# MLP up projections with the activations stationary, and a transposition by 32x32 blocks and DMAs

## The chip, the cores and the metric

The kernel runs on one core of one Trainium2 chip. The metric is the device time of one execution in microseconds; lower is better.

## The reference

A decoder trunk of two layers on 256 tokens of width 2048, all in float32. Layer 0 mixes with a gated linear recurrence and dilated window attention, layer 1 with differential attention. Each mixer is followed by a squared-ReLU MLP with 8192 hidden features; after each of the four sublayers comes a layer norm:

```
def squared_relu_mlp(x, w1, w2):
    h = jax.nn.relu(x @ w1)
    return (h * h) @ w2

for layer in range(DEPTH):
    ...
    x = layer_norm(ALPHA * x + mix, ln_mix_g[layer], ln_mix_b[layer])
    x = layer_norm(ALPHA * x + squared_relu_mlp(x, mlp_w1[layer], mlp_w2[layer]), ln_mlp_g[layer], ln_mlp_b[layer])
```

## The kernel before, in words

Every large product is made of three products of rounded parts. Each operand is split into a high part (the value in the matmul's float32r form) and a low part (the rest), and high x high, high x low and low x high are summed. The activations stand in SBUF with features on partitions: `xT` for the sublayer's input and `yT` for what the output products read, each with high and low parts. The first half of `yT` is `hT`, the hidden features of one block; the second half, `hT_last`, takes those of the last block.

All weights stream from HBM in blocks. A block has 8 chunks, a chunk is 256 rows by 512 columns. SyncE loads two chunks with one DMA of 1 MB into `raw`, which holds 8 chunks (`load`, line 267); the load waits until VectorE has made the low part of the chunks that lay there (`s_lo`). ScalarE makes the high part of a chunk (`split_hi`, line 364), VectorE the low part (`split_lo`, line 986), into rings of 4 chunks, `w_hi` and `w_lo`. So the high part of a chunk can be made once TensorE has finished the chunk four before it (`s_used`).

TensorE takes a chunk in one of two forms. `turned_chunk` (lines 674 and 678) holds 128x128 pieces of the weights stationary: 8 matmuls with 512 moving columns (high and low parts of the 256 tokens together) into four PSUM banks and 8 with 256 columns. Its result has features on partitions, in two halves (columns 0 to 255 and 256 to 511 of a bank) that still have to be added. `natural_chunk` (lines 700 to 702) holds 128 tokens of the activations stationary and moves 512 weight columns: 12 matmuls into two banks, one for each 128 tokens. Its result has tokens on partitions.

The MLP has 16 pairs of blocks in each layer: an up block (512 hidden features, `turned_chunk`) and a down block (`natural_chunk`, which adds the 512 features' share to all 2048 outputs). The order is up(0), then up(i+1), down(i) for i = 0 to 14, then down(15). It is written out by hand, the same for all engines: ScalarE and VectorE walk through the chunks k = 2 to 17 of up(i+1) and down(i) (`up_down`), some chunks ahead of TensorE, and other work is put at fixed k. When up(i+1) is done (k = 9), ScalarE copies the right halves from PSUM into `cross` (`copy_cross`), VectorE adds the left halves into `qs` (`add_cross`) and squares with ReLU (`squared`). At k = 4 of the next round `hidden_hi` (ScalarE, line 571) and `hidden_lo` (VectorE, line 1390) split `qs` into `hT`, before TensorE reaches the down block (chunks k = 8 to 15 of the round). After each quarter of a down block VectorE adds two banks to the residual `res` (line 1058). The first up block of a layer stands in `lead`, among the transpositions of the new `xT`. An engine executes its instructions in order, so whatever stands behind a waiting instruction waits too; this holds for SyncE's loads.

Of the kernel before, what the change touches and what calls it, by code (L numbers as in the profile page):

```python
# [70 lines left out]
GROUPS = D // CN  # L71


T_M0 = 8
T_OIN = T_M0 + FB
T_M1 = T_OIN + 2 * GROUPS


N_EOUT = 0
# [64 lines left out]
def build(nc, x, positions, ev_w_in, ev_conv_w, ev_conv_b, ev_gate_a_w, ev_gate_a_b, ev_gate_x_w,  # L144
# [11 lines left out]
    with ExitStack() as ctx:  # L156
# [3 lines left out]
        def sem(name):  # L160
# [34 lines left out]
        ln_x = ks[:].rearrange("p a s -> p (a s)").rearrange("p (b n) -> p b n", b=2)  # L195
        hT, hT_last = yT[:, 0:4], yT[:, 4:8]

        ln_par, rnn_par = rg[:, 0, 0, 0:P], rg[0:64, 0, 1, 0:P]
        pos, ang, turns = (rg[0:ROT, 1, n] for n in range(3))
        lam_vec = rg[:, 2]  # L200
# [29 lines left out]
        s_bn, s_k8, s_var, s_std, s_shift = (  # L230
            sem("block_statistics"), sem("softplus_made"), sem("variance"),
            sem("std"), sem("shift"))
        s_sq, s_hhi, s_hlo = sem("hidden_squared"), sem("hidden_hi"), sem("hidden_lo")
        s_S, s_neg, s_exp, s_P, s_T, s_pT, s_O = (sem("scores"), sem("neg_max"), sem("exps"), sem("probs"),
                                                  sem("probs_turned"), sem("probs_turned_copied"),
# [26 lines left out]
        @block.sync  # L262
        def _(sp):
            def load(blk, q, src):

                sp.wait_ge(s_lo, (blk - 1) * BLK + (2 * q + 2))
                sp.dma_start(raw[:, 2 * q:2 * q + 2].rearrange("p k t c -> p (k t) c"), src).then_inc(s_raw[q], 16)

            xv = x[0].rearrange("(t p) n -> p t n", p=P)
            sp.dma_start(cst[:, 0:P], consts[:, 0:P]).then_inc(s_id, 16)  # L270
            for k in range(BLK):
                cols = slice(k * CK * P, (k + 1) * CK * P)
                sp.dma_start(res[:, :, cols], xv[:, :, cols]).then_inc(s_x[k], 16)
                first = w_ein[k // 2, EVEN_IN_COLS[0]][:, k % 2 * CK:k % 2 * CK + CK]
                sp.dma_start(raw[:, k], first).then_inc(s_first[k], 16)
            sp.dma_start(cst[:, P:K_W], consts[:, P:K_W]).then_inc(s_cst, 16)
            for b, col in enumerate(EVEN_IN_COLS[1:], 1):
                for q in range(PAIRS):
                    load(B_EIN + b, q, w_ein[q, col])

            def load_out(order, blk, w):
                for n, (nb, kp, _, _) in enumerate(order[::2]):
                    load(blk + n // PAIRS, n % PAIRS, w[kp // 2, nb])

            def mlp(layer, b0):
                def up(blk, b):
                    for q in range(PAIRS):
                        load(blk, q, w_m1[layer][q, b])

                def down(blk, b):  # L290
                    for q in range(PAIRS):
                        load(blk, q, w_m2[layer][b, q])
                up(b0, 0)
                with sp.Fori(0, FB - 1) as i:
                    up(i * 2 + (b0 + 1), i + 1)
                    down(i * 2 + (b0 + 2), i)
                down(b0 + 2 * FB - 1, FB - 1)
# [57 lines left out]
        def _(act):  # L355
# [206 lines left out]
            layer_norm(0)  # L562


            def mlp(n, t0, b0):

                def hidden_hi(b, dst=hT):
                    act.wait_ge(s_sq, b + 1)
                    if dst is hT:
                        act.wait_ge(s_used, last_down(b))  # L570
                    nc.scalar.activation(dst[:, :, 0], qs[:], ACT.Copy).then_inc(s_hhi, 1)
# [5 lines left out]
                copy_cross(b0, t0)  # L577

                def up_down(i, last=False):

                    blk = i * 2 + (b0 + 1)
                    for k in range(2, 18):
                        split_hi(blk, k)
                        if k == 4:
                            hidden_hi(i + h0)
                        if k == 9:
                            copy_cross(blk, i + (t0 + 1))
                        if k == 12 and last:
                            hidden_hi(i + h0 + 1, hT_last)
# [12 lines left out]
            mlp(0, T_M0, B_M0)  # L602


            def odd_exps(idx):
# [54 lines left out]
                split_hi(B_OOUT, k)  # L660
                odd_events(k, 14, 12)
            layer_norm(2)
            mlp(2, T_M1, B_M1)


        @block.tensor
        def _(pe):
# [81 lines left out]
            def lead(n, blk, t):  # L749

                if n == 0:
                    ahead = 2
# [95 lines left out]
            for n, (nb, kp, first, last) in enumerate(EVEN_OUT):  # L848
# [1 line left out]
                    pe.wait_ge(s_v, 2)  # L850
                    pe.wait_ge(s_ylo, H_DIL)
                if first and nb == 1:
                    pe.wait_ge(s_turned, 2 * T_M0)
# [10 lines left out]
                even_events(B_EOUT * BLK + n)  # L864


            def mlp(n, t0, b0, n0):
                h0 = FB * (n // 2)

                def up(blk, t):  # L870
                    for k in range(BLK):
                        turned_chunk(blk, k, t)
# [13 lines left out]

                lead(n + 1, b0, t0)
                with pe.Fori(0, FB - 1) as i:
                    up(i * 2 + (b0 + 1), i + (t0 + 1))
# [3 lines left out]
            mlp(0, T_M0, B_M0, N_M0)  # L893


            def odd_scores(idx, hh, g):
# [65 lines left out]
            last_group = GROUPS - 1  # L962
            for n, (nb, kp, first, last) in enumerate(ODD_OUT):
                if n == 0:
                    pe.wait_ge(s_turned, 2 * T_M1)
# [10 lines left out]
            mlp(2, T_M1, B_M1, N_M1)  # L976


        @block.vector
        def _(dve):  # L980
# [394 lines left out]
            layer_norm(0, B_M0 * BLK)  # L1375


            def mlp(n, t0, b0, n0):
                h0 = FB * (n // 2)

                def squared(t):

                    add_cross(t, qs)
                    dve.wait_ge(s_turned, t * 2 + 2)
                    nc.vector.scalar_tensor_tensor(out=flat(qs[:]), in0=flat(qs[:]), scalar=0.0, in1=flat(qs[:]),
                                                   op0=ALU.max, op1=ALU.mult).then_inc(s_sq, 1)

                def hidden_lo(b, dst=hT):
                    dve.wait_ge(s_hhi, b + (h0 + 1))
                    nc.vector.tensor_tensor(dst[:, :, 1], qs[:], dst[:, :, 0].bitcast(F32), ALU.subtract).then_inc(s_hlo, 1)  # L1390
# [6 lines left out]
                squared(t0)  # L1397

                def up_down(i, last=False, first=False):

                    blk = i * 2 + (b0 + 1)
                    for k in range(2, 18):
                        split_lo(blk, k)
                        if k == 4:
                            hidden_lo(i)
                        if k == 9:
                            squared(i + (t0 + 1))
                        if first and k in (6, 8, 12, 14):
                            gain_residual(n, (6, 8, 12, 14).index(k))
                        if k == 12 and last:  # L1410
                            hidden_lo(i + 1, hT_last)
                        if k in (11, 13, 15, 17):
                            if first:
# [19 lines left out]
                else:  # L1433
                    last_layer_norm()

            mlp(0, T_M0, B_M0, N_M0)


            def odd_softmax(idx):
# [91 lines left out]
            mlp(2, T_M1, B_M1, N_M1)  # L1531


INPUTS = ["x", "positions", "ev_w_in", "ev_conv_w", "ev_conv_b", "ev_gate_a_w", "ev_gate_a_b", "ev_gate_x_w",
# [18 lines left out]
```

## Time and profile before

| | |
|---|---|
| median of 3 runs | 2177.41 us (2177.38 to 2177.56) |
| profiled execution, span | 2175.0 us |
| TensorE matmul busy | 2149.4 us, 99% |
| weight load busy (beside matmuls) | 1839.0 us, 85% |
| VectorE busy | 1431.8 us, 66% |
| ScalarE busy | 1021.6 us, 47% |
| DMA | 409.05 MB, mean 188 GB/s |

The span runs from the first to the last instruction of the one profiled execution; the timed runs last a little longer, since they include what lies around it. Busy shares of TensorE are of pipelined instructions, whose ends are modelled: the distance from one start to the next tells more than the duration. The page's `L` numbers are lines of the kernel.

### The profile page before, as it was taken

To read this page: it belongs to the slowest core of one execution; us is meant where nothing else is said; L and a number is where in the kernel's file an instruction comes from. 1 tells how busy PE (TensorE), PEld (TensorE's weight loads), DVE (VectorE), ACT (ScalarE), POOL (GpSimd) and SP (SyncE) were. 2 spreads that over 40 slices of the span, in tenths; PEclk is the share of its full clock that TensorE was granted. 3 is DMA by queue.
4 is the path that set the end of the run, shared out by engine and by line. 5 is a ranking of instruction groups with operands and counts; after the bars stand their busy time and mean duration, and the time that the engine had idled before them with its cause. 6 is when DMAs were issued, how large, how long until landed. Compare 5 with 4: busy or idle time off the path is not lost.

```text
span 2175.0 us, 29150 instructions
## 1 busy us (share of the span) xinstructions
PE 2149.4 (99%) x11058; PEld 1839.0 (85%) x11058; DVE 1431.8 (66%) x1480; ACT 1021.6 (47%) x1224; POOL 28.5 (1%) x38
## 2 busy tenths in 40 slices
PE   8999999999999999999999999999999999999997
PEld 7888888888888888888888888888888888888886
DVE  6776666756665666566787666567656665666667
ACT  4446656444444444444545545554444444444443
POOL 2000000000000000000000000000000000000002
PEclk9999999999999999999999999999999999999998
DMA  8555564655555555555564554555655555555552
GB/s 279 178 171 167 179 235 155 232 193 189 188 196 186 186 193 193 193 179 197 165 224 158 188 166 173 175 173 183 226 191 186 197 190 194 176 194 191 193 193 97
DMA packets 203809, 409.05 MB, mean 188 GB/s; under 512 B 6800, under 2 KB 9088, under 8 KB 202736
## 3 DMA queue, kind: packets, MB, share of 16 engines
q1 hardware_dynamic: 201920, 398.94, 54.8%
q0 software_dynamic: 1840, 9.44, 1.3%
q8 instruction: 32, 0.52, 0.1%
q14 instruction: 17, 0.14, 0.0%
HBM read 406.26 MB, written 2.10 MB: 188 GB/s over the span
## 4 chain that ended last, share of the span: by engine, by line
PE 97%; DVE 1%; DMA 1%; ACT 0%; SPq 0%; issue 0%
PE ps L674 32%; PE ps L678 17%; PE ps L701 15%; PE ps L700 15%; PE ps L702 15%; DMA raw<-in_ev_w_in 1%; PE ps L772 0%; PE ps L740 0%; PE ps L813 0%; PE ps L720 0%; PE ps L719 0%; PE ps L718 0%; PE ps L771 0%; PE ps L776 0%; DVE res L1106 0%; DVE stats L1072 0%
## 5 line engine op out<-in xcount | busy, mean ns | idle before, releaser
L364 ACT ACTIVATE w_hi<-raw 128x1024 fp32r<-128x1024 f32 x752 | 790.1, 1059 | 819.5 <-PE ps L702 479.4
L986 DVE TENSOR_TENSOR w_lo<-raw,w_hi 128x1024 fp32r<-128x1024 f32 x752 | 902.4, 1220 | 347.7 <-ACT w_hi L364 347.5
L674 PE MATMUL ps<-xT,w_hi 128*128 128x512 f32 x3072 | 769.5, 394 | 3.9 <-DVE xT L1016 3.6
L674 PEld LDWEIGHTS ps<-xT,w_hi 128*128 128x128 f32 x3072 | 557.0, 189 | 108.0 <-DVE xT L1016 4.6
L700 PE MATMUL ps<-w_hi,yT 128*128 128x512 f32 x1240 | 484.1, 390 | 0.0
L701 PE MATMUL ps<-w_lo,yT 128*128 128x512 f32 x1240 | 482.8, 389 | 0.0
L702 PE MATMUL ps<-w_hi,yT 128*128 128x512 f32 x1240 | 482.5, 389 | 0.0
L678 PEld LDWEIGHTS ps<-xT,w_lo 128*128 128x128 f32 x3072 | 408.7, 190 | 23.9
L678 PE MATMUL ps<-xT,w_lo 128*128 128x256 f32 x3072 | 420.2, 283 | 0.0
L1058 DVE TENSOR_TENSOR res<-ps,res 128x1024 f32<-128x1024 f32 x131 | 160.3, 1224 | 187.9 <-PE ps L702 187.9
L700 PEld LDWEIGHTS ps<-w_hi,yT 128*128 128x128 f32 x1240 | 232.7, 188 | 48.8
L702 PEld LDWEIGHTS ps<-w_hi,yT 128*128 128x128 f32 x1240 | 232.7, 188 | 48.6
L701 PEld LDWEIGHTS ps<-w_lo,yT 128*128 128x128 f32 x1240 | 232.8, 188 | 48.3
L993 DVE TENSOR_TENSOR qs<-ps,cross 128x512 f32<-128x512 f32 x76 | 52.6, 692 | 112.4 <-ACT cross L374 88.1
L374 ACT ACTIVATE cross<-ps 128x512 f32<-128x512 f32 x48 | 28.7, 598 | 142.1 <-PE ps L674 142.1
L700 PE MATMUL ps<-w_hi,xT 128*128 128x512 f32 x192 | 75.9, 395 | 0.0
L702 PE MATMUL ps<-w_hi,xT 128*128 128x512 f32 x192 | 74.8, 390 | 0.0
L701 PE MATMUL ps<-w_lo,xT 128*128 128x512 f32 x192 | 74.8, 390 | 0.0
L376 ACT ACTIVATE cross<-ps 128x512 f32<-128x512 f32 x48 | 28.7, 597 | 35.7 <-PE ps L674 35.7
L702 PEld LDWEIGHTS ps<-w_hi,xT 128*128 128x128 f32 x192 | 36.0, 188 | 7.7
L700 PEld LDWEIGHTS ps<-w_hi,xT 128*128 128x128 f32 x192 | 36.1, 188 | 7.5
L701 PEld LDWEIGHTS ps<-w_lo,xT 128*128 128x128 f32 x192 | 36.1, 188 | 7.4
(180 smaller groups left out, 826.2 us busy)
## 6 DMA issues: line engine op xcount, KB each, us to landing
raw<-in_mlp_w SPq DMA_DIRECT2D x256, 1024.0 KB, 5.0
raw<-in_od_w_in SPq DMA_DIRECT2D x48, 1024.0 KB, 5.1
raw<-in_ev_w_in SPq DMA_DIRECT2D x36, 1024.0 KB, 5.1
raw<-in_ev_w_out SPq DMA_DIRECT2D x16, 1024.0 KB, 5.0
raw<-in_od_w_out SPq DMA_DIRECT2D x16, 1024.0 KB, 5.0
raw<-in_ev_w_in SPq DMA_DIRECT2D x8, 512.0 KB, 11.8
res<-in_x SPq DMA_DIRECT2D x8, 256.0 KB, 9.7
rg<-in_ln_mix_g POOLq DMA_DIRECT2D x2, 1024.0 KB, 5.0
```

Source lines behind the costliest of these rows:

```text
L364: nc.scalar.activation(flat(w_hi[:, k % NSPL]), flat(raw[:, k % NRAW]), ACT.Copy).then_inc(s_hi, 1)
L374: nc.scalar.activation(cross[:, 0:2], ps[:, 0:2, S:2 * S], ACT.Copy).then_inc(s_cross, 1)
L376: nc.scalar.activation(cross[:, 2:4], ps[:, 2:4, S:2 * S], ACT.Copy).then_inc(s_cross, 1)
L674: return nc.tensor.matmul(ps[:, f], w_hi[:, k % NSPL, i, f * P:f * P + P], both, start=k == 0 and i == 0, stop=k == BLK - 1 and i == CK - 1)
L678: return nc.tensor.matmul(ps[:, f, S:2 * S], w_lo[:, k % NSPL, i, f * P:f * P + P], xT[:, CK * k + i, 0], start=False, stop=False)
L700: nc.tensor.matmul(bank, src[:, kt + i, 0, toks], hi, start=(start and i == 0), stop=False)
L701: nc.tensor.matmul(bank, src[:, kt + i, 0, toks], lo, start=False, stop=False)
L702: ins = nc.tensor.matmul(bank, src[:, kt + i, 1, toks], hi, start=False, stop=(stop and i == CK - 1))
L986: nc.vector.tensor_tensor(flat(w_lo[:, k % NSPL]), flat(raw[:, k % NRAW]), flat(w_hi[:, k % NSPL]).bitcast(F32), ALU.subtract).then_inc(s_ ...
L993: nc.vector.tensor_tensor(dst[:, 2 * h:2 * h + 2], ps[:, 2 * h:2 * h + 2, 0:S], cross[:, 2 * h:2 * h + 2], ALU.add).then_inc(s_turned, 1)
L1058: nc.vector.tensor_tensor(res[:, :, nb * CN:nb * CN + CN], ps[:, pair[0]:pair[0] + 2], res[:, :, nb * CN:nb * CN + CN], ALU.add).then_inc( ...
```

## The change

The up blocks of both MLPs use `natural_chunk` with `xT` stationary, into banks 0 and 1 (in `lead` into banks 2 and 3). The result now has tokens on partitions and hidden features along them, while the down product needs features on partitions. VectorE turns all 32x32 blocks of the two banks with one transpose instruction into `cross` (`blocks_turned`); each 32x32 block is then right in itself but stands in the wrong group of 32 partitions. SyncE exchanges the groups with 16 DMAs from SBUF to SBUF, `cross` to `ks` (`move_hidden`): each goes from one group of 32 partitions to one group, with 1 KB for each partition, written as two pieces of 512 B. Then VectorE squares `ks` into `qs`, and `hidden_hi` and `hidden_lo` split `qs` as before, reading it in pieces of 32 elements.

In the order of the work: `copy_cross` and `add_cross` go from the MLP. `blocks_turned` stands at k = 9. `move_hidden(i)` stands in SyncE's queue behind the first of the four loads of down(i). `squared(i)` moves to k = 4 of the round that has down(i), and waits there for the 16 DMAs; `hidden_hi` and `hidden_lo` move to k = 5. For the last block `squared` stands at k = 12 and the two splits at k = 13. TensorE waits before the seventh chunk of a down block until the newest block has been turned.

```
 # SyncE
+                def move_hidden(b):
+
+                    sp.wait_ge(s_block_tr, b + (layer * FB + 1))
+                    for a in range(NQ):
+                        for c in range(NQ):
+                            sp.dma_start(tiles_moved[QUAD * c:QUAD * c + QUAD, :, a],
+                                         tiles_turned[QUAD * a:QUAD * a + QUAD, c]).then_inc(s_moved, 16)
+
                 def down(blk, b):
                     for q in range(PAIRS):
                         load(blk, q, w_m2[layer][b, q])
+                        if q == 0:
+                            move_hidden(b)
 # ScalarE
                     for k in range(2, 18):
                         split_hi(blk, k)
-                        if k == 4:
+                        if k == 5:
                             hidden_hi(i + h0)
-                        if k == 9:
-                            copy_cross(blk, i + (t0 + 1))
-                        if k == 12 and last:
+                        if k == 13 and last:
                             hidden_hi(i + h0 + 1, hT_last)
 # TensorE
-                def up(blk, t):
+                def up(blk):
                     for k in range(BLK):
-                        turned_chunk(blk, k, t)
+                        natural_chunk(blk, k, (0, 1), xT, CK * k, k == 0, k == BLK - 1)
...
+                        if k == 6 and src is hT:
+                            pe.wait_ge(s_block_tr, b + (h0 + 2))
 # VectorE
-                def squared(t):
-
-                    add_cross(t, qs)
-                    dve.wait_ge(s_turned, t * 2 + 2)
-                    nc.vector.scalar_tensor_tensor(out=flat(qs[:]), in0=flat(qs[:]), scalar=0.0, in1=flat(qs[:]),
+                def blocks_turned(blk, bank):
+
+                    dve.wait_ge(s_used, blk * BLK + BLK)
+                    nc.vector.transpose(tiles_turned.rearrange("p c t f i -> p (t f) c i"),
+                                        ps[:, bank:bank + 2].rearrange("p t (f c j) -> p (t f) c j", c=NQ, j=QUAD)
+                                        ).then_inc(s_block_tr, 1)
+
+                def squared(b):
+
+                    dve.wait_ge(s_moved, (b + (h0 + 1)) * (16 * NQ * NQ))
+                    nc.vector.scalar_tensor_tensor(out=flat(qs[:]), in0=flat(ks[:]), scalar=0.0, in1=flat(ks[:]),
                                                    op0=ALU.max, op1=ALU.mult).then_inc(s_sq, 1)
...
                         split_lo(blk, k)
                         if k == 4:
+                            squared(i)
+                        if k == 5:
                             hidden_lo(i)
                         if k == 9:
-                            squared(i + (t0 + 1))
+                            blocks_turned(blk, 0)
```

## Rows read from the trace of the kernel before

**Rows 1.** The page: TensorE's busy line, and engines of the chain that ended last.

```profile
PE 2149.4 (99%) x11058; PEld 1839.0 (85%) x11058; DVE 1431.8 (66%) x1480; ACT 1021.6 (47%) x1224; POOL 28.5 (1%) x38
...
PE 97%; DVE 1%; DMA 1%; ACT 0%; SPq 0%; issue 0%
```

**Rows 2.** Windows view, five MLP rounds: busy of PE, PEld, DVE, ACT, POOL; granted clock; DMA.

```profile
424.15:644.49 220.34, 220.34 (x1122) 188.39 (x1121) 136.67 (x120) 94.54 (x96) 0.00 (x0) 1.00 0.59 196
```

**Rows 3.** The page, group: busy, mean ns | idle before it, and what ended it.

```profile
L674 PE MATMUL ps<-xT,w_hi 128*128 128x512 f32 x3072 | 769.5, 394 | 3.9 <-DVE xT L1016 3.6
```

**Rows 4.** Timeline of TensorE, a down block: start, duration; 17 threes of matmuls apart.

```profile
799.86 0.39 PE L700 MATMUL ps<-w_hi,yT 128*128 128x512 f32 x1
...
811.42 0.39 PE L700 MATMUL ps<-w_hi,yT 128*128 128x512 f32 x1
```

**Rows 5.** Timeline of TensorE, one whole up block and the next down block's start.

```profile
816.86 1.07 PE L674 MATMUL ps<-xT,w_hi 128*128 128x512 f32 x4
...
820.59 3.82 PE L674 MATMUL ps<-xT,w_hi 128*128 128x512 f32 x16
824.24 2.08 PE L678 MATMUL ps<-xT,w_lo 128*128 128x256 f32 x16
826.15 3.82 PE L674 MATMUL ps<-xT,w_hi 128*128 128x512 f32 x16
...
839.14 0.39 PE L700 MATMUL ps<-w_hi,yT 128*128 128x512 f32 x1
```

**Rows 6.** Chain of waits: start, duration; the same place of two rounds, five apart.

```profile
424.15 3.65 PE ps L674 x16
...
644.49 3.65 PE ps L674 x16
```

**Rows 7.** Timeline of TensorE, a natural block that reads xT, 25 threes apart.

```profile
1189.31 0.40 PE L700 MATMUL ps<-w_hi,xT 128*128 128x512 f32 x1
...
1206.34 0.39 PE L700 MATMUL ps<-w_hi,xT 128*128 128x512 f32 x1
```

**Rows 8.** Timeline of VectorE in the up block: k = 4, then the hidden low part.

```profile
820.93 1.23 DVE L986 TENSOR_TENSOR w_lo<-raw,w_hi 128x1024 fp32r<-128x1024 f32 x1 [0.38 <-ACT w_hi L364]
822.07 1.22 DVE L1390 TENSOR_TENSOR yT<-qs,yT 128x1024 fp32r<-128x1024 f32 x1
```

**Rows 9.** Timeline of ScalarE in the up block: k = 3, and the hidden high part.

```profile
817.12 1.06 ACT L364 ACTIVATE w_hi<-raw 128x1024 fp32r<-128x1024 f32 x1 [1.72 <-PE ps L702]
...
820.80 1.04 ACT L571 ACTIVATE yT<-qs 128x1024 fp32r<-128x1024 f32 x1
```

**Rows 10.** Timeline of SyncE: loads 1 and 2 of the down block, start and issue time.

```profile
815.28 0.37 SPq L267 DMA_DIRECT2D raw<-in_mlp_w  x1
...
820.71 0.37 SPq L267 DMA_DIRECT2D raw<-in_mlp_w  x1
```

**Rows 11.** Timeline of SyncE at the kernel's start, where DMAs are issued without waits.

```profile
1.19 0.42 SPq L273 DMA_DIRECT2D res<-in_x  x1
1.66 0.46 SPq L275 DMA_DIRECT2D raw<-in_ev_w_in  x1
...
3.75 0.76 SPq L275 DMA_DIRECT2D raw<-in_ev_w_in  x1
4.54 0.50 SPq L273 DMA_DIRECT2D res<-in_x  x1
```

**Rows 12.** DMA view of 0.7 to 2.0 us: packets, MB, share; issue's size, us to landing.

```profile
q1 hardware_dynamic: 56, 0.03, 10.6%
...
cst<-consts SPq DMA_DIRECT2D x1, 64.0 KB, 1.9
```

**Rows 13.** The page: landing of the MLP's loads.

```profile
raw<-in_mlp_w SPq DMA_DIRECT2D x256, 1024.0 KB, 5.0
```

**Rows 14.** Groups by line and shape, VectorE: the square, and the shuffle of partitions.

```profile
L1385 DVE SCALAR_TENSOR_TENSOR qs<-qs 128x1024 f32<-128x1024 f32 x32 | 39.2, 1225 | 1.1
...
L1002 DVE STREAM_SHUFFLE cross<-qs 32x1024 f32<-32x1024 f32 x6 | 8.0, 1338 | 0.0
```

More of the change, by code:

```diff
@@ L71 @@
 GROUPS = D // CN
-T_M0 = 8
-T_OIN = T_M0 + FB
-T_M1 = T_OIN + 2 * GROUPS
+T_OIN = 8
+T_OOUT = T_OIN + 2 * GROUPS
+QUAD = 32
+NQ = P // QUAD
 N_EOUT = 0
@@ L196, in build @@
         hT, hT_last = yT[:, 0:4], yT[:, 4:8]
+        tiles_turned = cross[:].rearrange("p a s -> p (a s)").rearrange("p (c t f i) -> p c t f i", c=NQ, t=TOK, i=QUAD)
+        tiles_moved = ks[:].rearrange("p a s -> p (a s)").rearrange("p (t a f i) -> p t a f i", t=TOK, a=NQ, i=QUAD)
+        hidden = qs[:].rearrange("p a s -> p (a s)").rearrange("p (n f i) -> p f n i", f=4, i=QUAD)
         ln_par, rnn_par = rg[:, 0, 0, 0:P], rg[0:64, 0, 1, 0:P]
@@ L232, in build @@
             sem("std"), sem("shift"))
+        s_block_tr, s_moved = sem("hidden_blocks_turned"), sem("hidden_blocks_moved")
         s_sq, s_hhi, s_hlo = sem("hidden_squared"), sem("hidden_hi"), sem("hidden_lo")
@@ L562, in _, with mlp @@
             layer_norm(0)
-            def mlp(n, t0, b0):
+            def mlp(n, b0):
                 def hidden_hi(b, dst=hT):
@@ L570, in hidden_hi @@
                         act.wait_ge(s_used, last_down(b))
-                    nc.scalar.activation(dst[:, :, 0], qs[:], ACT.Copy).then_inc(s_hhi, 1)
+                    nc.scalar.activation(dst[:, :, 0].rearrange("p f (n i) -> p f n i", i=QUAD), hidden,
+                                         ACT.Copy).then_inc(s_hhi, 1)
                 h0 = FB * (n // 2)
@@ L600, in mlp @@
                 layer_norm(n + 1)
-            mlp(0, T_M0, B_M0)
+            mlp(0, B_M0)
             def odd_exps(idx):
@@ L662, in _ @@
             layer_norm(2)
-            mlp(2, T_M1, B_M1)
+            mlp(2, B_M1)
         @block.tensor
@@ L747, in keep_busy, with lead @@
                     nc.tensor.matmul(ps[:, 0, 0:P], ident, ident, start=True, stop=True)
-            def lead(n, blk, t):
+            def lead(n, blk, t=None):
                 if n == 0:
@@ L765, in lead @@
                     pe.wait_ge(s_xlo, 8 * n + k + 1)
-                    turned_chunk(blk, k, t)
+                    if n % 2 == 0:
+                        turned_chunk(blk, k, t)
+                    else:
+                        natural_chunk(blk, k, (2, 3), xT, CK * k, k == 0, k == BLK - 1)
                     if k + ahead < 8:
@@ L852, in _ @@
                 if first and nb == 1:
-                    pe.wait_ge(s_turned, 2 * T_M0)
+                    pe.wait_ge(s_turned, 2 * T_OIN)
                 if kp == 0 and nb == 0:
@@ L864, in _, with mlp @@
                 even_events(B_EOUT * BLK + n)
-            def mlp(n, t0, b0, n0):
+            def mlp(n, b0, n0):
                 h0 = FB * (n // 2)
-                def up(blk, t):
+                def up(blk):
                     for k in range(BLK):
-                        turned_chunk(blk, k, t)
+                        natural_chunk(blk, k, (0, 1), xT, CK * k, k == 0, k == BLK - 1)
                 def down(blk, b, src=hT, whole=4):
@@ L885, in down @@
                                                for nb in range(whole, 4) for half in range(2)])
-                lead(n + 1, b0, t0)
+                lead(n + 1, b0)
                 with pe.Fori(0, FB - 1) as i:
-                    up(i * 2 + (b0 + 1), i + (t0 + 1))
+                    up(i * 2 + (b0 + 1))
                     down(i * 2 + (b0 + 2), i)
                 down(b0 + 2 * FB - 1, FB - 1, hT_last, whole=3 if n == 0 else 2)
-            mlp(0, T_M0, B_M0, N_M0)
+            mlp(0, B_M0, N_M0)
             def odd_scores(idx, hh, g):
@@ L964, in _ @@
                 if n == 0:
-                    pe.wait_ge(s_turned, 2 * T_M1)
+                    pe.wait_ge(s_turned, 2 * T_OOUT)
                     pe.wait_ge(s_ylo, H_DIL + 2 * last_group)
@@ L975, in _ @@
                 odd_events(n, H_DIL + 2 * last_group, last_group)
-            mlp(2, T_M1, B_M1, N_M1)
+            mlp(2, B_M1, N_M1)
         @block.vector
@@ L1375, in _, with mlp @@
             layer_norm(0, B_M0 * BLK)
-            def mlp(n, t0, b0, n0):
+            def mlp(n, b0, n0):
                 h0 = FB * (n // 2)
-                def squared(t):
-                    add_cross(t, qs)
-                    dve.wait_ge(s_turned, t * 2 + 2)
-                    nc.vector.scalar_tensor_tensor(out=flat(qs[:]), in0=flat(qs[:]), scalar=0.0, in1=flat(qs[:]),
+                def blocks_turned(blk, bank):
[6 more added lines that the diff above has]
+                    nc.vector.scalar_tensor_tensor(out=flat(qs[:]), in0=flat(ks[:]), scalar=0.0, in1=flat(ks[:]),
                                                    op0=ALU.max, op1=ALU.mult).then_inc(s_sq, 1)
@@ L1389, in hidden_lo @@
                     dve.wait_ge(s_hhi, b + (h0 + 1))
-                    nc.vector.tensor_tensor(dst[:, :, 1], qs[:], dst[:, :, 0].bitcast(F32), ALU.subtract).then_inc(s_hlo, 1)
+                    hi, lo = (dst[:, :, h].rearrange("p f (n i) -> p f n i", i=QUAD) for h in range(2))
+                    nc.vector.tensor_tensor(lo, hidden, hi.bitcast(F32), ALU.subtract).then_inc(s_hlo, 1)
                 def add_down(blk, b, nb):
@@ L1396, in mlp @@
                 lead(n + 1, b0)
-                squared(t0)
+                blocks_turned(b0, 2)
                 def up_down(i, last=False, first=False):
@@ L1410, in up_down @@
                         if k == 12 and last:
+                            squared(i + 1)
+                        if k == 13 and last:
                             hidden_lo(i + 1, hT_last)
@@ L1434, in mlp @@
                     last_layer_norm()
-            mlp(0, T_M0, B_M0, N_M0)
+            mlp(0, B_M0, N_M0)
             def odd_softmax(idx):
@@ L1530, in _ @@
             layer_norm(2, B_M1 * BLK)
-            mlp(2, T_M1, B_M1, N_M1)
+            mlp(2, B_M1, N_M1)
 INPUTS = ["x", "positions", "ev_w_in", "ev_conv_w", "ev_conv_b", "ev_gate_a_w", "ev_gate_a_b", "ev_gate_x_w",
```

1 line of the change is left out of this document (removed).

## The prediction

> **What bounds the kernel now.** I read the engine lines first, then the chain of waits, then one MLP round engine by engine. TensorE is busy 99% of the span and holds 97% of the chain that ended last [rows 1]; five MLP rounds in the middle show it busy for all of 220.34 us at a granted clock of 1.00, the 2.4 GHz level, with VectorE busy 62% and ScalarE 43% of that time [rows 2]. Before the heavy products of the turned form it sat idle for 3.9 us in the whole span [rows 3]. So time is won only where TensorE's stream of matmuls gets shorter, and lost only where something arrives after TensorE's turn. Everything that is taken from ScalarE and VectorE is worth nothing by itself.
>
> **TensorE's stream.** The reader is to look at distances between starts, not durations. In a down block 17 threes of 512-column matmuls take 811.42 - 799.86 = 11.56 us [rows 4], so one matmul takes 226.7 ns and a natural chunk of 12 takes 2.72 us, a block 8 x 2.72 = 21.76 us. In an up block 16 heavy products take 824.24 - 820.59 = 3.65 us, 228 ns each, and 16 light ones (256 columns) 826.15 - 824.24 = 1.91 us, 119 ns each [rows 5]. A turned chunk has 8 of each: 1.825 + 0.955 = 2.78 us. The columns are as many in both forms (8 x 512 + 8 x 256 = 12 x 512 = 6144), but two light products take 239 ns where one heavy one takes 227. The round gives the same from outside: 644.49 - 424.15 = 220.34 us for five rounds, 44.07 us each [rows 6]; less 21.76 for the down block, the up block takes 22.31 us. The one that I followed lasts 839.14 - 816.86 = 22.28 us [rows 5]. As a natural block it takes 21.76 us. That natural chunks keep this pace with xT stationary is seen in the value blocks of the odd mixer: 25 threes in 1206.34 - 1189.31 = 17.03 us, 227.1 ns a matmul [rows 7], which over 96 matmuls would be 0.04 us more for a block. The saving is 22.31 - 21.76 = 0.55 us a block, at least 22.28 - 21.80 = 0.48. There are 32 up blocks: 32 x 0.55 = 17.6 us, at least 15.4. I take 17.2 us, a little under the round's figure, since the two blocks in `lead` stand among transpositions.
>
> A page of the Trainium skill, "TensorE: Matmul & The Clock Gate" (Back-to-back issue gap), speaks against this. It gives the distance at 2.4 GHz as the columns' time plus about 2.5 ns a matmul, so 216 ns for 512 columns and 109 for 256. By it a turned chunk would take 8 x 216 + 8 x 109 = 2600 ns and a natural one 2592, and 256 chunks would save 2 us. The trace disagrees: what a matmul costs beyond its columns is 13 ns here, and the trace decides [rows 4, 5].
>
> **What must arrive in time.** I call the start of the up block T, 816.86 in the round of [rows 5]. The ring of splits has 4 chunks, so TensorE stops when the low part of chunk 5 isn't there at T + 5 x 2.72 = T + 13.6. In the new order VectorE makes the low part of chunk 4, waits for the 16 moves, squares (1.22 us [rows 14]) and makes the low part of chunk 5 (1.22 [rows 8]). So the moves must have landed by T + 13.6 - 2.44 = T + 11.15. (The old chunk 4 ended at 820.93 + 1.23 = T + 5.3 [rows 8], so up to there VectorE doesn't even wait.) The high part of the hidden block takes 1.04 us on ScalarE [rows 9] and the low part 1.22 on VectorE [rows 8]; they now stand behind chunk 5. Moves that land at T + 11.15 would put them at about T + 14.8, and the down block needs them at T + 21.76. Chunk 6 then ends at T + 16.0 and is needed at T + 16.3. That deadline is no tighter.
>
> When do they land? SyncE issues the first load of the down block at 815.28, T - 1.58 [rows 10]; the newest use of the hidden block's `cross` was turned a block earlier, so the wait in front of the moves costs nothing in a steady round. The moves follow it. At the kernel's start SyncE issues DMAs without waits, and the distance from one to the next is 0.47 us (1.19 to 1.66) while the queues are still empty, and 0.79 us (3.75 to 4.54) when they are full [rows 11]; the issue itself shows 0.37 us in the MLP [rows 10]. The trace of before has no DMA from SBUF to SBUF. I take 0.47 for each, bounds 0.37 and 0.79. A DMA of 64 KB lands 1.9 us after its issue [rows 12]; I take that for a move of 32 KB. So the last one is issued at T - 1.11 + 15 x 0.47 = T + 5.9 and has landed at T + 7.8, 3.3 us before the deadline. The data themselves: 56 packets, nearly all of 512 B, took 10.6% of 16 engines in 1.3 us, 39 ns each [rows 12]. The moves have 16 x 64 = 1024 such packets, and with 256 semaphore writes counted alike 1280 x 39 / 16 = 3.1 us, behind the load that lands 5.0 us after its issue [rows 13]: T + 3.4 + 3.1 = T + 6.5. So the issue limits, not the data, and the steady rounds pay nothing.
>
> Queued behind the moves in SyncE are loads 2 to 4 of the down block. Load 2 was issued at 820.71, T + 3.85 [rows 10], and now at T + 6.4; it lands at T + 11.4. ScalarE wants it for the third chunk of the down block, which it starts when TensorE starts chunk 7, at T + 19.0. That hides 2.5 us with 7.6 us left. No one else waits for SyncE.
>
> **The four edge rounds.** In the first round of each layer the block is turned only when `lead` has ended, at T + 0.2, and the moves start at about T + 1.6: the last lands at T + 1.6 + 15 x 0.47 + 1.9 = T + 10.6, against a deadline of T + 11.15 less about 0.6 for the residual's gain that stands behind chunk 6 there. For the last block the moves start 1.6 us after its up block has ended and VectorE waits at k = 12, with chunk 13 needed 5 chunks, 13.6 us, after that end: the same sum. I take 0.1 us a place, 0.4 in all; bounds 0 and, at 0.55 us a move, 1.2 each, 4.8 in all.
>
> **The rest.** The transpose reads 128x1024 of PSUM on VectorE, in the place of two additions. No row shows one; the nearest are 1.22 us for an instruction of that shape [rows 14] and 1.34 for the shuffle of partitions [rows 14]. I take 1.3, bounds 1.2 and 2.7. It starts when the up block ends, and chunk 10 (1.22) is needed 5.44 us after that, so up to 4.0 us of it is hidden. The splits now read pieces of 32 elements; taken at their old 1.04 and 1.22 us, hidden even when doubled, by the 6.9 us before the down block. TensorE's new wait, before the seventh chunk of a down block, asks for a transposition that ended 13 us earlier: nothing. ScalarE's and VectorE's removed copies and additions lie beside TensorE: nothing.
>
> Sum: 2175.0 - 17.2 + 0.4 = 2158.2 us of span. The timed median, 2177.4, is 2.4 above the span, so 2160.6 us.
>
> **The rivals.**
> (a) The moves land too late. Mechanism: SyncE issues one after the other and VectorE stands behind the last, so with distance s they land at T - 1.11 + 15 s + 1.9. TensorE stops in each of 28 to 30 steady rounds once s is above 0.69 us. At 0.79 the last lands at T + 12.6, 1.5 us late: 30 x 1.5 = 45 us, and at the four edges 1.6 + 11.85 + 1.9 = T + 15.4, 4.3 us late: 17 us. 2160.2 + 62 = 2222 us. It decides from 0.70 us a move: above that the kernel is slower than before. For it speak the full queues at the start, and that each moving DMA has two access patterns in SBUF; against it, that the queues here hold one load only, and that a load of 512 packets shows 0.37 us of issue.
> (b) The moves don't overlap each other. Each then pays its 1.9 us after the one before: 16 x 1.9 = 30.4 us, landing at T + 29, 18 us late in 30 rounds, 2700 us. Against it: at the start DMAs land in 1.9 us and more while they are issued every 0.47 us. The Trainium skill leans this way in "DMA: Bandwidth & Descriptors" (Rules for kernel authors): transfers under 64 KB pay mostly overhead, and its table (Bandwidth) has 0.95 us for 64 KB; were the moves to follow each other at nearly that, 16 x 0.8 = 12.8 us behind the load, they would land at T + 16 and cost an estimated 5 us a round. No run here shows it yet.
> (c) The moves are late by little, at 0.69 to 0.70 us or by some hundreds of ns of extra latency: 0.2 us a round and 1.5 at each edge, 12 us, 2172 us.
> (d) Nothing is won, since the natural up block runs at 232 ns a matmul (22.31 us over 96): 2177. The page on TensorE above would give 2175. Against it [rows 4, 7].
>
> **How the numbers follow.** Forecast 0.78, (a) 0.10, (b) 0.02, (c) 0.07, (d) 0.03. The likeliest case reaches from 2158.5 (0.57 us a block, edges free) to 2166 (15.4 saved, edges at 4.8, rounded up). The range reaches towards (c): 2158 to 2170. A measurement of this kernel tells 0.2%, 4.4 us, from no change: faster 0.84 (the forecast and most of (c)), same 0.04, slower 0.12.
>
> **What would show it.** Right: starts in an up block 226.7 ns apart throughout, a round of 43.5 us, no idle time of TensorE in steady rounds, SyncE's 16 issues in 7 to 8 us, VectorE's transpose under 4 us. Wrong: VectorE waiting at the square for a DMA until after T + 11.15, TensorE idle before chunk 5 of an up block (a), (b), (c); or up blocks still above 22 us without idle time (d). A granted clock under 1.00 anywhere in the MLP would void the whole sum.

## The result and the profile after

| | median | runs | profiled span |
|---|---|---|---|
| before | 2177.36 us | 20 (2176.38 to 2178.96) | 2175.0 us |
| changed | 2174.36 us | 20 (2172.97 to 2176.2) | 2172.3 us |

The ratio is 0.9986, 95% interval 0.9981 to 0.9992: faster by 3 us, where 16.8 were forecast. From the page of the changed kernel: the engines' busy time, the chain that ended last, the matmuls of the natural form that read `xT`, the two new groups of VectorE, and the moves.

```profile
PE 2135.4 (98%) x10034; PEld 1786.2 (82%) x10034; DVE 1418.1 (65%) x1448; ACT 983.6 (45%) x1160; POOL 28.5 (1%) x38
...
PE 91%; DVE 4%; SPq 3%; DMA 1%; issue 1%; ACT 0%; DVEq 0%
...
L714 PE MATMUL ps<-w_hi,xT 128*128 128x512 f32 x1216 | 476.4, 392 | 7.1 <-DVE w_lo L1005 4.9
...
L1410 DVE SCALAR_TENSOR_TENSOR qs<-ks 128x1024 f32<-128x1024 f32 x32 | 39.2, 1225 | 172.5 <-DMA ks<-cross 172.5
...
L1403 DVE STREAM_TRANSPOSE cross<-ps 128x1024 f32<-128x1024 f32 x32 | 40.0, 1249 | 92.7 <-PE ps L716 92.7
...
ks<-cross SPq DMA_DIRECT2D x512, 32.0 KB, 1.9
```

TensorE's busy time fell by 14.0 us, and its share of the chain fell from 97% [rows 1] to 91%: VectorE, SyncE's issues and the moves have entered it, and TensorE now waits for `w_lo` where it never did. VectorE waits 172.5 us for the moves, 5.4 us before each of the 32 squares.

A steady round first. TensorE's timeline at the starts of an up block (line 714 with `xT`), its down block (`yT`) and the next up block:

```profile
816.99 0.39 PE L714 MATMUL ps<-w_hi,xT 128*128 128x512 f32 x1
...
838.75 0.39 PE L714 MATMUL ps<-w_hi,yT 128*128 128x512 f32 x1
...
860.50 0.39 PE L714 MATMUL ps<-w_hi,xT 128*128 128x512 f32 x1
```

21.76 us each, 43.51 in all, against 22.28 for the up block [rows 5] and 44.07 for the round [rows 6]. VectorE and SyncE in the same round:

```profile
821.00 1.23 DVE L1005 TENSOR_TENSOR w_lo<-raw,w_hi 128x1024 fp32r<-128x1024 f32 x1 [0.32 <-ACT w_hi L380]
827.32 1.22 DVE L1410 SCALAR_TENSOR_TENSOR qs<-ks 128x1024 f32<-128x1024 f32 x1 [5.09 <-DMA ks<-cross]
828.46 1.22 DVE L1005 TENSOR_TENSOR w_lo<-raw,w_hi 128x1024 fp32r<-128x1024 f32 x1
```

```profile
815.82 10.20 SPq L301 DMA_DIRECT2D ks<-cross  x16
```

16 moves fill 10.20 us, 0.64 us each. The last has landed at 827.3, T + 10.3, and the deadline was T + 11.15: the steady rounds are in time by 0.8 us. Issue and landing are two things here. The first move of this round, issued at 815.82 right behind a load of 1 MB, lands late, 5.0 us after its issue; the moves behind it land sooner and sooner, and the last eight 1.8 to 1.9 us after theirs:

```profile
ks<-cross SPq DMA_DIRECT2D x1, 32.0 KB, 5.0
```

Now the first round of layer 0. The chain of waits across it (start, duration), from the last issue of a move on:

```profile
388.24 0.60 SPq L301
388.84 0.04 issue
388.88 1.83 DMA ks<-cross
390.72 0.02 issue
390.74 1.22 DVE qs L1410
391.96 1.15 DVE w_lo L1005
393.11 0.04 issue
393.15 0.50 PE ps L714
```

And TensorE there, then the windows view of 380 to 400 us, where 0.91 is the granted clock's mean:

```profile
389.95 0.39 PE L716 MATMUL ps<-w_hi,xT 128*128 128x512 f32 x1
393.15 0.50 PE L714 MATMUL ps<-w_hi,xT 128*128 128x512 f32 x1 [2.82 <-DVE w_lo L1005]
393.49 0.56 PE L715 MATMUL ps<-w_lo,xT 128*128 128x512 f32 x1
393.85 0.63 PE L716 MATMUL ps<-w_hi,xT 128*128 128x512 f32 x1
394.28 0.63 PE L714 MATMUL ps<-w_hi,xT 128*128 128x512 f32 x1
...
397.13 0.39 PE L715 MATMUL ps<-w_lo,xT 128*128 128x512 f32 x1
```

```profile
380.00:400.00 20.00, 17.18 (x69) 13.76 (x68) 10.72 (x10) 6.58 (x7) 0.00 (x0) 0.91 0.41 130
```

The last move lands and VectorE squares, makes the low part of chunk 5, and only then TensorE goes on. Behind the idle stretch the matmuls stand 0.43 us apart, not 0.227: the granted clock has fallen to its 1.2 GHz level, and it is back after 3.4 us, which costs 1.7 us more. (Line 714 starts 3.2 us behind the matmul before it, 3.0 more than the usual 0.23: 3.0 and 1.7 are the 4.7 us of "first 0" below.)

From here on the kernels are compared by stretches between first matmuls, in us. "First" is `lead` and up(1) of a layer, "second" the next up block (up(2)), "last" the two down blocks that end layer 0 with the layer norm behind them, "end" the same of layer 1 up to the end of the span.

| | first 0 | second 0 | last 0 | first 1 | second 1 | end 1 | steady up block |
|---|---|---|---|---|---|---|---|
| before | 46.84 | 22.28 | 49.71 | 46.82 | 22.28 | 57.4 | 22.28 |
| changed | 50.29 | 22.28 | 52.36 | 47.92 | 22.35 | 60.7 | 21.76 |
| no moves | 45.59 | 21.76 | 49.68 | 45.61 | 21.76 | 58.0 | 21.76 |
| two places later | 45.65 | 21.76 | 49.68 | 45.61 | 21.76 | 58.0 | 21.76 |
| edges later | 45.61 | 22.54 | 49.69 | 45.59 | 22.65 | 58.0 | 21.76 |
| one place later | 47.89 | 21.76 | 50.01 | 46.80 | 21.76 | 58.4 | 21.76 |
| one piece | 49.69 | 22.81 | 52.23 | 47.81 | 22.41 | 60.6 | 21.76 |
| HBM source | 46.11 | 22.81 | 49.74 | 45.63 | 22.19 | 58.1 | 21.76 |
| all partitions | 48.35 | 22.47 | 52.30 | 47.88 | 22.43 | 60.6 | 21.76 |
| half by GpSimd | 45.59 | 22.11 | 49.69 | 47.58 | 22.09 | 64.4 | 21.76 |
| twenty moves | 53.27 | 26.04 | 56.55 | 51.66 | 26.11 | 64.0 | 23.55 to 23.70 |

### The profile page after: what moved, and what is told of

The parts are those of the page before. It is cut to its first block, busy times and chain, and to the rows that moved or that the text cites. A ratio compares the mean times of both kernels' runs of the same rounds, so it can differ in the third digit from the quotient of the medians.

```text
span 2172.3 us, 27393 instructions
## 1 busy us (share of the span) xinstructions
PE 2135.4 (98%) x10034; PEld 1786.2 (82%) x10034; DVE 1418.1 (65%) x1448; ACT 983.6 (45%) x1160; POOL 28.5 (1%) x38
## 4 chain that ended last, share of the span: by engine, by line
PE 91%; DVE 4%; SPq 3%; DMA 1%; issue 1%; ACT 0%; DVEq 0%
PE ps L714 24%; PE ps L716 24%; PE ps L715 24%; PE ps L688 10%; PE ps L692 5%; SPq L301 3%; DVE w_lo L1005 1%; DMA raw<-in_ev_w_in 1%; DMA ks<-cross 1%; PE ps L789 0%; DVE res L1077 0%; PE ps L754 0%; PE ps L830 0%; DVE res L1068 0%; PE ps L734 0%
## 5 line engine op out<-in xcount | busy, mean ns | idle before, releaser
L714 PE MATMUL ps<-w_hi,xT 128*128 128x512 f32 x1216 | 476.4, 392 | 7.1 <-DVE w_lo L1005 4.9
L716 PE MATMUL ps<-w_hi,xT 128*128 128x512 f32 x1216 | 474.0, 390 | 0.0
L715 PE MATMUL ps<-w_lo,xT 128*128 128x512 f32 x1216 | 473.9, 390 | 0.0
L714 PEld LDWEIGHTS ps<-w_hi,xT 128*128 128x128 f32 x1216 | 228.7, 188 | 56.8 <-DVE w_lo L1005 7.2
L716 PEld LDWEIGHTS ps<-w_hi,xT 128*128 128x128 f32 x1216 | 228.6, 188 | 47.9
L715 PEld LDWEIGHTS ps<-w_lo,xT 128*128 128x128 f32 x1216 | 228.7, 188 | 47.1
L688 PE MATMUL ps<-xT,w_hi 128*128 128x512 f32 x1024 | 261.9, 397 | 1.8 <-DVE xT L1035 1.5
L688 PEld LDWEIGHTS ps<-xT,w_hi 128*128 128x128 f32 x1024 | 185.0, 189 | 36.6 <-DVE xT L1035 2.0
L1410 DVE SCALAR_TENSOR_TENSOR qs<-ks 128x1024 f32<-128x1024 f32 x32 | 39.2, 1225 | 172.5 <-DMA ks<-cross 172.5
L692 PEld LDWEIGHTS ps<-xT,w_lo 128*128 128x128 f32 x1024 | 137.4, 190 | 9.6 <-DVE xT L1035 1.1
L692 PE MATMUL ps<-xT,w_lo 128*128 128x256 f32 x1024 | 143.7, 284 | 0.9 <-DVE xT L1035 0.9
L1403 DVE STREAM_TRANSPOSE cross<-ps 128x1024 f32<-128x1024 f32 x32 | 40.0, 1249 | 92.7 <-PE ps L716 92.7
## 6 DMA issues: line engine op xcount, KB each, us to landing
raw<-in_ev_w_in SPq DMA_DIRECT2D x8, 512.0 KB, 12.4
```

What stands on the lines that cost most here:

```text
L688: return nc.tensor.matmul(ps[:, f], w_hi[:, k % NSPL, i, f * P:f * P + P], both, start=k == 0 and i == 0, stop=k == BLK - 1 and i == CK - 1)
L692: return nc.tensor.matmul(ps[:, f, S:2 * S], w_lo[:, k % NSPL, i, f * P:f * P + P], xT[:, CK * k + i, 0], start=False, stop=False)
L714: nc.tensor.matmul(bank, src[:, kt + i, 0, toks], hi, start=(start and i == 0), stop=False)
L715: nc.tensor.matmul(bank, src[:, kt + i, 0, toks], lo, start=False, stop=False)
L716: ins = nc.tensor.matmul(bank, src[:, kt + i, 1, toks], hi, start=False, stop=(stop and i == CK - 1))
L1403: nc.vector.transpose(tiles_turned.rearrange("p c t f i -> p (t f) c i"), ps[:, bank:bank + 2].rearrange("p t (f c j) -> p (t f) c j", c=N ...
```

## The experiments

Ratios are to the kernel before. The stretch ahead of the first MLP differs by up to 2.6 us from profile to profile (`lead` of layer 0 begins 351.6 to 354.2 us into the span, behind the same work), so that profiles of two kernels are compared by the table and not by their spans.

**Without the moves.** The exchange is left out; `squared` reads `cross` once it has been turned.

```
-                        if q == 0:
-                            move_hidden(b)
...
-                    dve.wait_ge(s_moved, (b + (h0 + 1)) * (16 * NQ * NQ))
+                    dve.wait_ge(s_block_tr, b + (h0 + 1))
```

> The 16 moves are left out, and the square reads the turned blocks where they stand (so the exchange of the partition groups is not computed). Theory A: the changed kernel takes 0.545 us from each of the 32 up blocks (17.4 us) and gives back about 13 us at the four edge rounds, where VectorE waits for the last move; without moves nothing is given back: 2160 us, no idle time of TensorE before a chunk of the MLP, granted clock 1.00 there. Theory B: the loss lies elsewhere (TensorE's new wait, the strided splits, the new lead): then this kernel stays at 2168 us or above and TensorE still idles in the MLP.

2160.99 us, ratio 0.9926 (0.9913 to 0.994). No wait of TensorE for a chunk is left in either MLP. The whole gain of the matmul form is there, and the changed kernel gave back 13.5 us of it: by the table 4.7 + 0.5 + 2.7 + 2.3 + 0.6 + 2.7, all in the edge rounds and those right behind the first.

**The square and the splits two places later.**

```
-                        if k == 4:
+                        if k == 6:
                             squared(i)
-                        if k == 5:
+                        if k == 7:
                             hidden_lo(i)
... (14 and 15 instead of 12 and 13 for the last block; hidden_hi likewise)
```

> The changed kernel whole, but the square at k = 6 instead of 4 (14 instead of 12 for the last block) and the two splits of the hidden block at k = 7 (15). The deadline for the last move becomes T + 16.6 instead of T + 11.15. Theory A: at 0.64 to 0.72 us a move the edge rounds land at T + 13 to T + 14.5, now in time: 2160 us, as without moves. Theory B1 (the 16 moves cost by themselves, through DMA traffic or SyncE's later loads): clearly above the kernel without moves. Theory B2 (the hidden splits come too late for the down block): TensorE idles before the first chunk of down blocks, over 2165 us.

2162.15 us, ratio 0.9932 (0.9918 to 0.9945). The moves are all there, and take as long as in the changed kernel; SyncE and VectorE in the first round of layer 0:

```profile
379.53 11.31 SPq L301 DMA_DIRECT2D ks<-cross  x16
```

```profile
387.50 1.23 DVE L1005 TENSOR_TENSOR w_lo<-raw,w_hi 128x1024 fp32r<-128x1024 f32 x1 [1.49 <-ACT w_hi L380]
392.10 1.22 DVE L1410 SCALAR_TENSOR_TENSOR qs<-ks 128x1024 f32<-128x1024 f32 x1 [3.37 <-DMA ks<-cross]
```

VectorE still waits 3.4 us there, but with two more chunks split ahead of the wait, and TensorE doesn't stop. The moves cost next to nothing by themselves: no stretch of the table differs from "no moves" by more than 0.06 us, and one down block (the first) by 0.26. This version beats both kernels: 15 us less than before. But it has less room than the T + 16.6 of the expectation: in the first round the residual's gain stands between the square and chunk 7, which is ready at 396.85, 0.2 us before TensorE starts on it.

**Only the edge rounds later.** As above, but the rounds between keep k = 4 and 5.

```
-                        if k == 4:
+                        if k == (6 if first else 4):
                             squared(i)
```

> Only the first round of each layer and the last block get the later places (square at k = 6 and splits at k = 7, 14 and 15 for the last block); the 14 rounds between keep the changed kernel's k = 4 and 5. Theory A (the loss is the late moves of the edge rounds): all but some tenths comes back, 2162 us; the second round of each layer, where the moves start 0.8 us late, may keep 0.5 us each. Theory C (the steady rounds lose as well): clearly slower than with all rounds late, 2165 us or more.

2162.47 us, ratio 0.993 (0.9917 to 0.9944), as theory A had it. The up block behind the first round keeps 0.8 to 0.9 us, more than the 0.5 expected; why is told with the HBM source below.

**One place later.**

```
-                        if k == 4:
+                        if k == 5:
                             squared(i)
-                        if k == 5:
+                        if k == 6:
                             hidden_lo(i)
... (13 and 14 for the last block; hidden_hi likewise)
```

> The square one place later than in the changed kernel (k = 5, 13 for the last), the splits at k = 6 (14), in all rounds: deadline T + 13.9. By theory A the last move of an edge lands at T + 13.1, in time, and in the very first edge (0.72 us a move) at T + 14.1, 0.2 us late: 2162 us. Theory D (the splits two places later were what helped, not the deadline): half of the gain, 2168 us.

2164.95 us, ratio 0.994 (0.9926 to 0.9953): neither number, and the deadline in the expectation was at fault. VectorE in the first round, and TensorE's wait:

```profile
390.31 1.22 DVE L1410 SCALAR_TENSOR_TENSOR qs<-ks 128x1024 f32<-128x1024 f32 x1 [6.09 <-DMA ks<-cross]
391.46 1.22 DVE L1005 TENSOR_TENSOR w_lo<-raw,w_hi 128x1024 fp32r<-128x1024 f32 x1
392.67 1.23 DVE L1416 TENSOR_TENSOR yT<-qs,yT 128x1024 fp32r<-128x1024 f32 x1
393.81 1.22 DVE L1068 SCALAR_TENSOR_TENSOR res<-res,rg 128x1024 f32<-128x1024 f32 x1
395.06 1.22 DVE L1071 SCALAR_TENSOR_TENSOR res<-rg,res 128x1024 f32<-128x1024 f32 x1
396.20 2.35 DVE L1005 TENSOR_TENSOR w_lo<-raw,w_hi 128x1024 fp32r<-128x1024 f32 x2
```

```profile
397.48 0.50 PE L714 MATMUL ps<-w_hi,xT 128*128 128x512 f32 x1 [1.73 <-DVE w_lo L1005]
```

Behind the square stand the low part of chunk 6, the hidden low part and, in the first round alone, the residual's gain; chunk 7 comes after them and is ready at 397.4, 7.1 us after the square's start. It is needed at T + 19.0, so the deadline there is T + 11.9 and not T + 13.9. A landing at T + 14.1 is 2.2 us late, and 47.89 - 45.59 = 2.3 was paid; in layer 1 a landing at T + 13.1 cost 1.2. At two places later the gain stands behind the square as well, but chunk 6 and the hidden low part no longer stand between the square and chunk 7.

**Twenty moves.** The four moves within a group are cut in two; the bytes are the same.

```
+                            for t in (range(TOK) if a == c else (slice(0, TOK),)):
+                                sp.dma_start(tiles_moved[QUAD * c:QUAD * c + QUAD, t, a],
+                                             tiles_turned[QUAD * a:QUAD * a + QUAD, c, t]).then_inc(s_moved, 16)
```

> The changed kernel with 20 moves: the four between equal groups are cut in two of half the size, same bytes. Theory A (a price per DMA issued): at 0.64 us each the last lands 2.6 us later, T + 12.9 in a steady round against a deadline of T + 11.15, 1.75 us late in 28 rounds and 2.6 more at the edges: 2174 + 49 + 10 = 2233 us. If the price is by packets or bytes, the last move lands when it did: 2174 us.

2245.02 us, ratio 1.0312 (1.0296 to 1.0328). A steady round: SyncE's issues, VectorE's square, TensorE's stop; and the sum of all such stops.

```profile
474.97 12.80 SPq L302 DMA_DIRECT2D ks<-cross  x20
```

```profile
488.99 1.22 DVE L1411 SCALAR_TENSOR_TENSOR qs<-ks 128x1024 f32<-128x1024 f32 x1 [7.61 <-DMA ks<-cross]
```

```profile
491.40 0.50 PE L715 MATMUL ps<-w_hi,xT 128*128 128x512 f32 x1 [1.51 <-DVE w_lo L1006]
```

```profile
PE ps L715 <- DVE w_lo L1006: 62.5, 32, 5.0
```

The price is by the DMA, 0.64 us each, half size or whole. Up blocks take 23.55 us in layer 0, 1.79 more than 21.76, against the 1.75 expected, and about 23.65 in layer 1: the deadline is where it was put, within 0.2 us. The 12 us beyond the expected total are in the second rounds (4.3 us each), in the edge rounds and in the up blocks of layer 1; the granted clock is at its lower level in six places behind longer stops, 3.4 or 6.8 us each time.

**The issue of a move by itself.** Three kernels change the moves alone.

```
# one piece: 1 KB for each partition on both sides
+        tiles_moved = ... .rearrange("p (a t f i) -> p a t f i", t=TOK, a=NQ, i=QUAD)
# HBM source: rows of w_m2, same destination; no exchange
+                            sp.dma_start(tiles_moved[QUAD * c:QUAD * c + QUAD, :, a].rearrange("p t f i -> p t (f i)"),
+                                         w_m2[layer][0, 0][QUAD * a:QUAD * a + QUAD, 0:TOK, P * c:P * c + P])
# all partitions: columns 64 n to 64 n + 63 of cross to the same of ks; no exchange
+                    for n in range(NQ * NQ):
+                        sp.dma_start(ks[...][:, 64 * n:64 * n + 64], cross[...][:, 64 * n:64 * n + 64])
```

> The moves write 1 KB in one piece for each partition, not two of 512 B; the square undoes the order in two instructions. Theory P (the distance of 0.64 us from move to move grows with the pieces or dimensions): it falls to 0.5 us or less, each edge gains about 2 us, 2167 us. Theory Q (it is a price of an instruction with both ends in SBUF, whatever its pieces): 0.64 us as before, 2174 us.

> The 16 moves read weights from HBM (2 x 128 floats for each of 32 rows) in place of the turned blocks, so the exchange is not computed; destination, size and number are the same. Theory Q (two ends in SBUF make the issue long): the distance falls from 0.64 to about 0.45 us, and the edges lose less, 2168 us. Theory R (the small partition range or the piece form of the destination makes it long): 0.64 us stays.

> 16 DMAs from SBUF to SBUF again and the same bytes, but each over all 128 partitions with one piece of 256 B for each, from the same columns to the same columns (so the exchange is not computed). With an HBM source the distance from issue to issue was 0.46 us, with an SBUF source 0.64. Theory Q (an SBUF source makes the issue long): 0.64 us again, 2174 us. Theory R (a small partition range in SBUF on both ends makes it long): under 0.5 us and 2163 us.

SyncE's 16 issues in one steady round of the changed kernel, of the HBM source, and of all partitions:

```profile
554.70 10.21 SPq L301 DMA_DIRECT2D ks<-cross  x16
```

```profile
507.41 7.55 SPq L301 DMA_DIRECT2D ks<-in_mlp_w  x16
```

```profile
554.30 10.17 SPq L300 DMA_DIRECT2D ks<-cross  x16
```

0.64, 0.47 and 0.64 us each. One piece: 2174.05 us, ratio 0.9985 (0.9976 to 0.9994), 0.63 us each. HBM source: one run of 2163.02 us. All partitions: one of 2174.07, beside 2176.55 for the kernel before. Neither pieces nor the range of partitions matter; a source in SBUF, with a destination in SBUF too, does. (No run has an SBUF source and another destination, so whether it takes both ends stays open.) With the shorter issue of an HBM source the edges are in time but for 0.5 us in the first round. One issue in the first batch of a run took 1.7 us in the changed kernel and 1.1 to 1.2 in these three; why is open, as is what makes an SBUF source dearer to issue.

The second rounds don't follow the issue distance: with the HBM source they lose 1.05 and 0.43 us, against 0.52 and 0.59 in the changed kernel. SyncE's load just ahead of the moves, the moves, and VectorE's square in the second round of layer 0, first of the changed kernel, then of the HBM source:

```profile
raw<-in_mlp_w SPq DMA_DIRECT2D x1, 1024.0 KB, 9.0
424.40 10.28 SPq L301 DMA_DIRECT2D ks<-cross  x16
436.35 1.23 DVE L1410 SCALAR_TENSOR_TENSOR qs<-ks 128x1024 f32<-128x1024 f32 x1 [6.32 <-DMA ks<-cross]
```

```profile
raw<-in_mlp_w SPq DMA_DIRECT2D x1, 1024.0 KB, 9.4
420.10 8.29 SPq L301 DMA_DIRECT2D ks<-in_mlp_w  x16
432.58 1.23 DVE L1410 SCALAR_TENSOR_TENSOR qs<-ks 128x1024 f32<-128x1024 f32 x1 [6.86 <-DMA ks<-in_mlp_w]
```

The load ahead of the moves lands 9.0 and 9.4 us after its issue, where it takes 5.3 in a steady round: two loads of 1 MB by GpSimd, the rows of the next layer norm, are under way there. The last move then lands 2.2 us after its issue in the changed kernel and 4.6 with the HBM source, where it was issued sooner. So the landing limits these rounds at least in part. That GpSimd's loads are the reason is read from the order of times; no run leaves them out.

**Half of the moves issued by GpSimd.**

```
+            def move_hidden(b, layer):
+                pool.wait_ge(s_block_tr, b + (layer * FB + 1))
+                for a in range(NQ // 2, NQ):
+                    for c in range(NQ):
+                        pool.dma_start(...).then_inc(s_moved_pool, 16)
```

> The changed kernel's places, but 8 of the 16 moves are issued by GpSimd, on its own queue. Theory A: SyncE has issued its 8 after 5.1 us, GpSimd at the 0.5 us an issue that it showed at the start after 4 us; the last lands 4 to 5 us earlier, unless GpSimd's moves land much later than SyncE's 1.9 us (at the start it was 5 us beside a full queue): T + 9 at the edges, in time, 2162 us. Rival: what limits is the DMA engines' work on small pieces, which stays: 2174 us.

2170.56 us, ratio 0.9969 (0.9957 to 0.998): half a miss. SyncE and GpSimd in the first round of layer 0, then GpSimd in that of layer 1:

```profile
377.94 5.23 SPq L302 DMA_DIRECT2D ks<-cross  x8
```

```profile
378.21 4.29 POOL L359 DMA_DIRECT2D ks<-cross  x8 [83.34 <-DVE cross L1419]
```

```profile
1477.72 1.06 POOL L359 DMA_DIRECT2D ks<-cross  x2 [2.61 <-issue]
```

The two queues do run side by side, and "first 0" is as short as without moves. But in layer 1 GpSimd paused 2.6 us between two issues, for nothing that the profile shows, and "first 1" kept 2.0 us; and the span's end is 6.4 us longer than without moves. Those 6.4 us stand behind the last computation, which ends at 2158.3. The program ends when GpSimd's closing DRAIN does; the groups of its last line have it at 11.5 us, and it takes 3.9 without moves and in the changed kernel:

```profile
L157 POOLq DRAIN  x1: 11517/11517/11517, 2156.1 to 2156.1; - x1
```

GpSimd's 256 issues are written out one by one; whether that or the moves themselves cause the pause and the long DRAIN was not tested.

## Why the prediction was wrong, point by point

- **TensorE's stream: right.** 0.55 us a block was taken; a steady round went from 44.07 to 43.51 us and up blocks stand at 21.76. Without the moves the kernel is 16 us faster, the forecast's 16.8 within its error. The idea that the two forms cost the same (d) is out. The trace, not the 2.5 ns a matmul of the Trainium skill's "TensorE: Matmul & The Clock Gate" (Back-to-back issue gap), was the one to follow; the page gives that figure for a matmul by itself, and its other one, about 131 ns for 512 columns in a sustained stream, isn't seen here either (227).
- **The issue distance: the step that failed.** The prediction took 0.47 us "for each, bounds 0.37 and 0.79", from loads whose source is HBM [rows 11]. That is what moves with an HBM source show (0.47). With both ends in SBUF it is 0.64, in the first batch 0.71. The value lay inside its bounds; taking the near row made the likeliest case too good, since that row differed from the new instruction in the one thing that counts. One of the prediction's own signs told it: 16 issues took 10.2 us, where 7 to 8 were named.
- **The steady rounds: right in outcome, with 0.8 us to spare where 3.3 were forecast.** The landing after the last issue (1.9 us) and the deadline T + 11.15 held; twenty moves found the deadline within 0.2 us.
- **The edges: the term of the sum that was mis-sized.** 0.4 us was taken, at most 4.8; they cost 12.4, and the second rounds, which the prediction counted as steady, 1.1 more. The same formula with 0.64 and 0.71 gives landings at T + 13.1 and T + 14.1; against T + 10.5 in the first rounds that is 2.6 and 3.6 us, against T + 11.15 at the last blocks 2.0 each: 10.2 of the 13.5 us. In the trace the stops before chunk 5 are 3.0, 1.8, 1.8 and 1.8 us. What stands behind the square (the residual's gain or an addition to the residual) delays a later chunk by 0.5 to 0.9 us more at three of the edges; at the first one no such delay is seen, where TensorE ran at the lower clock. What the formula lacked: 1.7 us for the clock that falls behind the longest stop, and the second rounds (0.5 and 0.6), where SyncE starts the moves 0.8 us later than in a steady round and the last one lands 2.2 us after its issue.
- **Bounds that didn't fit together.** The issue distance was given up to 0.79 us, but the edges' bound of 4.8 us was worked out at 0.55; at 0.64 the prediction's own formula says about 9 us. And the lower end, 2158.5, should read 2159.2 by its own terms (32 blocks at 0.57 us), the upper one 2166.8.
- **The rivals.** (a) and (c) had the right mechanism, and (c) the nearest number, 2172 us; but (c) was tied to 0.69 us and to steady rounds that are late, and got 7%. That its number comes near is partly luck: it priced an edge at 1.5 us, where its own 0.69 us a move puts the landing 2.7 us late or more. A case "0.6 to 0.69, edges alone late" was missing, and so the range ended at 2170, 4 us short of 2174.4. (b) is out: in a steady round all 16 moves have landed 11.5 us after the first issue. The estimate that the prediction made from the Trainium skill's "DMA: Bandwidth & Descriptors" (Rules for kernel authors, Bandwidth), some 5 us lost in a round, didn't come either: the moves overlapped, and the last eight landed 1.9 us after their issue, though issued every 0.64 us.
- **The transpose, the strided splits, SyncE's later loads, TensorE's new wait: right.** The transpose takes 1.25 us against 1.3 taken, and the kernel with the square two places later shows none of the four in TensorE's waits.

## What to carry to other kernels

When a chain of small DMAs comes between a product and its use, price it as count times issue distance, and take the distance from a DMA with the same kinds of ends. Then look for the rounds that are not steady: there the chain starts later, more work stands behind the wait, and other transfers may be under way; a few such rounds can eat what the steady ones save. The cure costs nothing if the wait can be moved a few places down its engine's queue, behind work that others need sooner: 2 places gave back 12 us by the medians, and all but 0.3 of the 13.5 us by the table. Look again at what then stands behind the wait: at one place it was chunk 7 that came too late, and at two it had 0.2 us left.

## What the runs showed of the hardware

- A DMA issued by SyncE with its source in SBUF keeps its queue 0.64 us, with its source in HBM 0.47 us, at 32 KB each; half the size, 256 B, 512 B or 1 KB pieces, 32 or 128 partitions change it by 0.02 us at most. Of the same moves GpSimd issued 8 in 4.29 us, 0.54 each.
- Of 16 moves of 32 KB issued every 0.64 us, the first, right behind a 1 MB load, landed 5.0 us after its issue and the last eight 1.8 to 1.9 us. In the second round, where that load took 9.0 us instead of 5.3, the last one took 2.2 us, and 4.6 with an HBM source.
- A matmul with 256 columns costs 119 ns and one with 512 costs 227 [rows 4, 5], so the form with fewer and longer matmuls takes 2.3% less time at equal columns (21.76 us a block against 22.28).
- VectorE's transpose of 128x1024 float32 from PSUM in 32x32 blocks takes 1.25 us, where the square and the splits of that shape take 1.22.
- In the changed kernel the granted clock stood at its 1.2 GHz level for 3.4 us behind the stop at 393 us (2.8 us idle); behind the other stops before a chunk (1.6 us idle at most) it stayed at 2.4 GHz.
- GpSimd's closing DRAIN took 11.5 us in the kernel in which it had issued 256 moves, and 3.9 us in the changed kernel.
